# Two late modulation rows summed 256 columns at a time in the gate units; block means transposed straight from the gate tile

## What is computed

```python
mod = silu(c) @ w_ada + b_ada                     # 6 rows of 1,024
shift1, scale1, gate1, shift2, scale2, gate2 = split(mod, 6)
h  = modulated_norm(x, norm_mix_g, shift1, scale1)
xr, gr, zu, zv, ga, gb = split(h @ w_in, ...)
y_a = (rg_lru(conv4(xr)) * gelu(gr)) @ w_branch_a
v   = layernorm(gelu(zv))                         # over the channels of a token
y_b = (gelu(zu) * (blockwise 128x128 masked position mixing of v + b)) @ w_branch_b
x   = x + gate1 * ((sigmoid(ga) * y_a + sigmoid(gb) * y_b) @ w_out)
h   = modulated_norm(x, norm_ffn_g, shift2, scale2)
x   = x + gate2 * ((gelu(a) * b) @ w_down)        # a, b: conv3 of h @ w_up
return rmsnorm(x, norm_final_g)
```

## Time and profile before

| | |
|---|---|
| median of three runs | 1533.09 us (1532.81 to 1533.11) |
| the profiled execution | 1533.34 us, of which its span is 1531.6 us |
| PE | 1510.5 us busy, 99% of the span |
| DVE | 1199.9 us, 78% |
| ACT | 811.6 us, 53% |
| POOL | 387.0 us, 25% |
| granted TensorE clock | full in all slices |

### The profile page before, as it was taken

The page is one execution under the profiler, slowest core; times in us unless marked ns, Lnnn a source line. Parts: engine busy times, 40 slices in busy tenths (PEclk is TensorE's granted clock), DMA queues, the critical chain, the costliest instruction groups (busy, mean ns, idle before and its releaser), DMA issues.

```text
span 1531.6 us, 19518 instructions
## 1 busy us (share of the span) xinstructions
PE 1510.5 (99%) x6820; PEld 1243.1 (81%) x6820; DVE 1199.9 (78%) x1484; ACT 811.6 (53%) x1207; POOL 387.0 (25%) x291
## 2 busy tenths in 40 slices
PE   7999999999999999999999999999999999999998
PEld 4778888888888888888887788888888888888887
DVE  6987888745565685478859999999999987777775
ACT  5378988745554460112535555655555553444447
POOL 0024334522222200000000333333333331333324
PEclk9999999999999999999999999999999999999999
DMA  9531233222332256674421144444444446777722
GB/s 347 182 104 49 82 90 91 86 66 71 111 103 83 97 169 225 185 241 134 165 62 35 49 151 165 152 151 151 152 151 152 151 131 230 242 249 249 248 66 111
DMA packets 199985, 219.56 MB, mean 143 GB/s; under 512 B 8944, under 2 KB 155728, under 8 KB 199120
## 3 DMA queue, kind: packets, MB, share of 16 engines
q1 hardware_dynamic: 199888, 218.32, 43.1%
HBM read 160.61 MB, written 57.67 MB: 143 GB/s over the span
## 4 chain that ended last, share of the span: by engine, by line
PE 90%; DVE 7%; ACT 1%; issue 1%; DMA 0%; DVEq 0%; ACTq 0%
PE ps L808 70%; PE ps L881 10%; PE ps L1159 1%; PE ps L1068 1%; PE ps L1011 1%; PE ps L1141 1%; PE ps L931 1%; DVE wop L1838 1%; PE ps L966 1%; DVE part_acc L1901 1%; DVE yq L1936 1%; DVE hidw L2481 1%; DVE tn L1931 1%; DVE yq L2424 1%; DVE n L2416 0%
## 5 line engine op out<-in xcount | busy, mean ns | idle before, releaser
L1222 ACT ACTIVATE wop<-raw 128x512 fp32r<-128x512 f32 (+1 forms) x529 | 299.4, 570 | 401.2 <-PE ps L808 209.9
L1838 DVE TENSOR_TENSOR wop<-raw,wop 128x512 fp32r<-128x512 f32 (+1 forms) x529 | 366.9, 697 | 163.0 <-ACT wop L1222 161.0
L808 PE MATMUL ps<-yq,wop 128*128 128x512 f32 x1680 | 404.6, 390 | 1.3 <-DVE wop L1838 0.9
L808 PEld LDWEIGHTS ps<-yq,wop 128*128 128x128 f32 x1680 | 314.8, 188 | 69.2 <-DVE yq L2424 1.6
L649 POOL TENSOR_TENSOR raw<-raw,raw 128x512 f32<-128x512 f32 (+1 forms) x65 | 95.7, 1472 | 925.3 <-DVE wop L1838 428.6
L808 PE MATMUL ps<-dq,wop 128*128 128x512 f32 x840 | 190.6, 389 | 0.0
L808 PEld LDWEIGHTS ps<-dq,wop 128*128 128x128 f32 x840 | 157.7, 188 | 32.7
L1852 DVE TENSOR_TENSOR ps<-ps,snap_p 128x512 f32<-128x512 f32 x128 | 89.0, 696 | 56.2 <-PE ps L808 55.5
L808 PE MATMUL ps<-t2q,wop 128*128 128x512 f32 x528 | 127.7, 391 | 1.1 <-DVE wop L1838 1.1
L808 PE MATMUL ps<-t4q,wop 128*128 128x512 f32 x528 | 127.2, 390 | 1.0 <-DVE ps L1852 1.0
L808 PE MATMUL ps<-t3q,wop 128*128 128x512 f32 x528 | 127.8, 391 | 0.0
(11 more groups left out here) (266 smaller groups left out, 1979.9 us busy)
## 6 DMA issues: line engine op xcount, KB each, us to landing
dq<-hid_keep SPq DMA_DIRECT2D x35, 1024.0 KB, 7.2
raw<-in_w_in SPq DMA_DIRECT2D x96, 256.0 KB, 3.9
raw<-in_w_up SPq DMA_DIRECT2D x96, 256.0 KB, 3.3
hid_keep<-part_b SPq DMA_DIRECT2D x40, 512.0 KB, 3.0
ada_ring<-in_w_ada SPq DMA_DIRECT2D x32, 512.0 KB, 4.4
hid_keep<-part_t SPq DMA_DIRECT2D x20, 512.0 KB, 2.8
raw<-in_w_down SPq DMA_DIRECT2D x80, 128.0 KB, 2.3
ada_w<-in_w_ada SPq DMA_DIRECT2D x8, 1024.0 KB, 11.5
```

Source lines behind the costliest of these rows:

```text
L808: done = nc.tensor.matmul(bank, left[:, w, lk, :], right[:, x, rk, :], start=(first and w == 0 and x == 0), stop=(last and w == 1), skip_g ...
L1222: nc.scalar.activation(wop[n % 4][:, 0, 0:depth[n], :], raw[slot][:, 0:depth[n], :], ACT.Copy).then_inc(f_hi, 1)
L1838: V.tensor_tensor(wop[n % 4][:, 1, 0:kd, :], raw[slot_of[n][0]][:, 0:kd, :], wop[n % 4][:, 0, 0:kd, :].bitcast(F32), ALU.subtract).then_in ...
```

## The change

Rows 0 and 1 are no longer made in `A` 1 and `A` 2. They are cut into eight parts ("quarters" of a row) of 256 columns, one for each unit with a block b. In unit j of these, DVE sums eight pieces of 128x256 (`quarter_piece`), one or two behind the `lo` of each step. They come from a ring of four buffers of 128 KB, which lie where `vstage` was. PE sums the partitions of the quarter after product 1 of the next unit (two matmuls of one column), DVE adds the bias at w = 3 (`quarter_columns`), and PE waits for that (`mod_ready`) before it mixes. The transposes read `vv` itself, so `stage` and `vstage` are gone. Rows 2 and 3 stay in `B` 0 and `B` 1. SP issues the pieces between weight and gate transfers, and the first return of `ya_raw` moves behind the first weights of `ZU` 3 and also waits for the last quarter.

```diff
-        ADA_AT = {AT["A", 1]: 0, AT["A", 2]: 1, AT["B", 0]: 2, AT["B", 1]: 3}
-        SUMS_AT = {AT["A", 2]: 0, AT["A", 3]: 1, AT["B", 1]: 2, AT["B", 3]: 3}
+        ADA_AT = {AT["B", 0]: 2, AT["B", 1]: 3}
+        SUMS_AT = {AT["B", 1]: 2, AT["B", 3]: 3}
+        QUARTER_AT = {pos: V_BLOCK[pos] for pos in V_BLOCK}
...
+            def quarter_pieces(j, *ks):
+                for k in ks:
+                    n = KT * j + k
+                    if n == 0:
+                        sp.wait_ge(scanned, KT)
+                    if n >= len(quarter_ring):
+                        sp.wait_ge(ring_used, n + 2 - len(quarter_ring))
+                    slot = n % len(quarter_ring)
+                    sp.dma_start(quarter_ring[slot][:, :], w_ada[:, k, 2 * D + j * QC:2 * D + (j + 1) * QC])\
+                      .then_inc(ring_landed[slot], 16)
...
-                weights(pos, 0, 4 if pos == 2 else 2)
+                weights(pos, 0, 1)
+                if now - 1 in QUARTER_AT:
+                    quarter_pieces(QUARTER_AT[now - 1], 7)
...
+                if now in QUARTER_AT:
+                    quarter_pieces(QUARTER_AT[now], 0, 1, 2)
+                weights(pos, 1, 4 if pos == 2 else 2)
...
+                if now in QUARTER_AT:
+                    quarter_pieces(QUARTER_AT[now], 3)
                 if pos > 2:
                     weights(pos, 3, 4)
+                if now in QUARTER_AT:
+                    quarter_pieces(QUARTER_AT[now], 4, 5, 6)
...
+                if pos - 1 in QUARTER_AT:
+                    j = QUARTER_AT[pos - 1]
+                    if w == 2:
+                        pe.wait_ge(*outputs_read(pos - 1, 1))
+                        pe.wait_ge(*quarter_used(j, KT - 1))
+                        column_sums(quarter_acc, QC // P, past[1][:, 0, 0:QC // P]).then_inc(ada_psum, 1)
+                    if w == 4:
+                        pe.wait_ge(mod_ready, j + 1)
...
-                        pe.wait_ge(staged, b + 1)
+                        if b == 0:
+                            pe.wait_ge(zv_ready, KT)
                         for g in range(G):
-                            last = nc.tensor.transpose(blocks(past[0])[:, g, :], vstage[:, g, :], ident[:, :])
+                            last = nc.tensor.transpose(blocks(past[0])[:, g, :], vv[:, g, b * P:(b + 1) * P], ident[:, :])
...
+            FIRST_OPS = ((), (0,), (1, 2), (3,), (4,), (5,), (6, 7))
+            QUARTER_OPS = ((0,), (1, 2), (3,), (4,), (5,), (6,), (7,))
+
+            def quarter_piece(j, k):
+                n = KT * j + k
+                w, before = quarter_ring[n % len(quarter_ring)], quarter_ring[(n - 1) % len(quarter_ring)]
+                dve.wait_ge(ring_landed[n % len(quarter_ring)], 16 * (n // len(quarter_ring) + 1))
+                if k == 0:
+                    V.tensor_scalar(w[:, :], w[:, :], cact[:, 0:1], None, ALU.mult).then_inc(ring_used, 1)
+                else:
+                    dve.wait_ge(*quarter_used(j, k - 1))
...
+                    dst = quarter_acc if k == KT - 1 else w
+                    V.scalar_tensor_tensor(dst[:, :], w[:, :], cact[:, k:k + 1], before[:, :], ALU.mult, ALU.add)\
+                     .then_inc(ring_used, 1)
...
+                    if pos - 1 in QUARTER_AT and w == 3:
+                        quarter_columns(QUARTER_AT[pos - 1], past[1])
                     if w or m is None:
                         lo(n0 + w + 3)
+                    if pos in QUARTER_AT:
+                        for k in (QUARTER_OPS if QUARTER_AT[pos] else FIRST_OPS)[w]:
+                            quarter_piece(QUARTER_AT[pos], k)
```

More of the change, by code:

```diff
@@ L157, in build @@
         sq_o = place("sq_o", [S], F32, "T", 2 * TILE)
-        ada_ring = [[place("ada_ring0", [D], F32, "X", 6 * TILE), place("ada_ring1", [D], F32, "T", 3 * TILE)],
-                    [place(f"ada_ring{2 + i}", [D], F32, "H", 3 * QUAD + at * TILE) for i, at in enumerate((0, 1, 3))]]
-        ada_acc = [place("ada_acc0", [D], F32, "X", 7 * TILE), place("ada_acc1", [D], F32, "H", 3 * QUAD + 2 * TILE)]
+        ada_ring = [place(f"ada_ring{i}", [D], F32, "H", 3 * QUAD + at * TILE) for i, at in enumerate((0, 1, 3))]
+        ada_acc = place("ada_acc", [D], F32, "H", 3 * QUAD + 2 * TILE)
+        QC = 2 * P
+        quarter_ring = [place(f"quarter_ring{i}", [QC], F32, "H", 3 * QUAD + i * 4 * QC) for i in range(4)]
+        quarter_acc = place("quarter_acc", [QC], F32, "BD", 2 * KB)
         n22, n12 = (place(n, [KH, HALF], F32, "H", (i + 1) * QUAD) for i, n in enumerate(("n22", "n12")))
@@ L263, in build @@
         r_psum, sbias_ready = sem("r_psum"), sem("sbias_ready")
-        staged, v_psum, var_ready, sd_ready, vhat_ready, mix_psum, mixed_ready, zu_ready, yb_ready = (
-            sem(x) for x in ("staged", "v_psum", "var_ready", "sd_ready", "vhat_ready", "mix_psum", "mixed_ready",
+        v_psum, var_ready, sd_ready, vhat_ready, mix_psum, mixed_ready, zu_ready, yb_ready = (
+            sem(x) for x in ("v_psum", "var_ready", "sd_ready", "vhat_ready", "mix_psum", "mixed_ready",
                              "zu_ready", "yb_ready"))
@@ L270, in build @@
             sem(x) for x in ("yb_hi", "yb_lo", "ma_done", "mb_done", "mg_hi", "mg_lo"))
-        ring_landed, ring_used = [sem(f"ring_landed{s}") for s in range(3)], sem("ring_used")
+        ring_landed, ring_used = [sem(f"ring_landed{s}") for s in range(4)], sem("ring_used")
         ada_sum, ada_psum, mod_ready = (
@@ L312, in build @@
         V_BLOCK = {AT["G", 2 + b] if b < 6 else AT["ZU", b - 6]: b for b in range(NB)}
-        ADA_AT = {AT["A", 1]: 0, AT["A", 2]: 1, AT["B", 0]: 2, AT["B", 1]: 3}
-        SUMS_AT = {AT["A", 2]: 0, AT["A", 3]: 1, AT["B", 1]: 2, AT["B", 3]: 3}
+        ADA_AT = {AT["B", 0]: 2, AT["B", 1]: 3}
+        SUMS_AT = {AT["B", 1]: 2, AT["B", 3]: 3}
+        QUARTER_AT = {pos: V_BLOCK[pos] for pos in V_BLOCK}
+        QUARTERS = 2 * D // QC
+        EARLY = KT * QUARTERS
+        assert QUARTERS == len(QUARTER_AT)
         def plain(item):
@@ L393, in ring_place, with quarter_used @@
         def ring_place(e, k):
-            n = KT * (e % 2) + k
-            slots = len(ada_ring[e // 2])
-            return n % slots, 16 * (n // slots + 1 + (KT if e >= 2 and n % slots < 2 else 0))
+            n = KT * (e - 2) + k
+            return n % len(ada_ring), 16 * (n // len(ada_ring) + 1 + EARLY // len(quarter_ring))
+        def quarter_used(j, k):
+            return ring_used, KT * j + k + 1
         def prev_unit(pos, kind, back=1):
@@ L523, in _ @@
                 now = pos - 1
-                weights(pos, 0, 4 if pos == 2 else 2)
+                weights(pos, 0, 1)
+                if now - 1 in QUARTER_AT:
+                    quarter_pieces(QUARTER_AT[now - 1], 7)
+                if SEQ[now - 1] == ("ZU", 1):
+                    sp.wait_ge(mixed_ready, NB)
+                    sp.wait_ge(ring_used, EARLY)
+                    sp.wait_ge(ya_spilled[0], 16 * KT // 2)
+                    sp.wait_ge(ya_spilled[1], 16 * KT // 2)
+                    sp.dma_start(ya_raw[0][:, :, :], ya_keep[:, 0:KH, :]).then_inc(kept_back[0], 16)
+                if now in QUARTER_AT:
+                    quarter_pieces(QUARTER_AT[now], 0, 1, 2)
+                weights(pos, 1, 4 if pos == 2 else 2)
                 g = prev_unit(now, "G")
@@ L536, in _ @@
                 if now in ADA_AT:
-                    ada_pieces(ADA_AT[now], len(ada_ring[ADA_AT[now] // 2]), 7 if ADA_AT[now] == 3 else 8)
+                    ada_pieces(ADA_AT[now], len(ada_ring), 7 if ADA_AT[now] == 3 else 8)
                 if SEQ[now] == ("B", 2):
@@ L556, in _ @@
                       .then_inc(ws_landed, 16)
[L557 to L561, removed]
                 if SEQ[now] == ("ZU", 3):
@@ L1498, in _ @@
                             gate_tanh(1, 1)
-                        if b is not None and b + 1 < NB:
-                            stage(b + 1)
                         if SEQ[pos] == ("ZU", 3):
@@ L2052, in scan, with quarter_columns @@
                 V.tensor_tensor_scan(ti[m % 2][:, :], la_a[:, :], ti[m % 2][:, :], 0.0, ALU.mult, ALU.add).then_inc(scanned, 1)
+            FIRST_OPS = ((), (0,), (1, 2), (3,), (4,), (5,), (6, 7))
[8 more added lines that the diff above has]
+                    dve.wait_ge(*quarter_used(j, k - 1))
+                    if k == KT - 1 and j:
+                        dve.wait_ge(ada_psum, j)
+                    dst = quarter_acc if k == KT - 1 else w
+                    V.scalar_tensor_tensor(dst[:, :], w[:, :], cact[:, k:k + 1], before[:, :], ALU.mult, ALU.add)\
+                     .then_inc(ring_used, 1)
+            def quarter_columns(j, bank):
+                n, c0 = QC // P, 2 * KT + QC // P * j
+                dve.wait_ge(ada_psum, j + 1)
+                V.tensor_tensor(mod[:, c0:c0 + n], bank[:, 0, 0:n], C("b_ada", c0, n), ALU.add).then_inc(mod_ready, 1)
             def v_stats(b, bank):
@@ L2229, in _ @@
                         e = ADA_AT[pos]
```

(3 more changed lines are left out.)

45 lines of the change are left out of this document (17 added, 28 removed).

## The result

The changed kernel takes 1538.19 us (median of six runs, 1536.49 to 1539.89) against 1533.05 us (six runs, 1532.81 to 1533.37). The ratio is 1.0033, with a 95% interval of 1.0023 to 1.0043: slower by 5.1 us, where 5.75 us were forecast. The spread is new: 3.4 us, where the kernel before has 0.6.

What follows compares the result with a forecast made beforehand. PE, busy throughout 93 to 806 us, was taken as the bound. Column sums 0.2, `G` 2 1.8 and three late pieces 3.75 sum to 5.75 us: 1538.8 us from the 1533.09 median, range 1534.5 to 1543.0.

Steps and rivals of the forecast that it cites:

- What bounds the kernel: From 93 to 806 us PE alone bounds; DVE work removed gives nothing, added costs nothing until PE waits.
- Staging copy: ACT loses eight copies, none on the chain, hidden by busy PE: nothing.
- Column sums: On PE, eight small sums of 0.48 us (3.9 us) replace two costing 3.70: net +0.2 taken, up to +1.0 us.
- the line that I drew: PE column-sum cost from two sizes: 0.114 us a record plus 0.03 fixed, so 0.48 us for 4 records.
- Pieces of 0.48 us: Each 256-column DVE piece takes 0.48 us; two in w = 1 delay the variance 0.9 us, hidden by the root's table load.
- `G` 2, 1.8 us: Two pieces ahead of `vhat`, the second held up by POOL at the port: PE waits 1.8 us.
- Late pieces: In the seven later units, piece 3 landing after its turn lets POOL in: 1.25 us each, three counted, 3.75 us.
- SP's queue and `ya_raw`: SP's waits for earlier pieces and the first `ya_raw` going out some 5 us later are hidden: nothing.
- B: Rival: all pieces land in time, only `G` 2 waits: 1535.1 us; chance 0.24.
- C: Rival: the piece loses the port to POOL in every later unit, even when landed: 1543.8 us; chance 0.14.
- D: Rival: pieces don't shut POOL out, `G` 2 costs 0.85 us: 1534.2 us in all; chance 0.06.
- the ring order: DMA engines take descriptors in ring order, so piece 3 stands behind 1 MB of gate tiles; landings of 5.0 to 6.2 us.

Runs made afterwards that it cites:

- the fourth experiment: Changed kernel with only the first unit's order changed, pieces 1 and 2 of `G` 2 moved behind `vhat`: 1535.99 us.
- the third experiment: Changed kernel with SP issuing piece 3 ahead of both gate tiles instead of behind them: 1535.18 us.
- fifth experiments: Changed kernel with piece 3 moved behind `vhat` in the seven later units, `G` 2 left as it is: 1535.06 us.
- the last two: Changed kernel with POOL's sums waiting for `vhat`: 1535.57 us; piece 3 issued early, plus pieces 2 and 3 ahead of `vhat` in seven later units: 1544.47 us.

## Why the prediction was right, point by point

- **What bounds the kernel.** It held: 16 pieces of 1,024 columns and eight ACT copies went and gave nothing, and in the version with all pieces behind `vhat` the new DVE work cost nothing.
- **Staging copy, nothing.** Measured at 0.9999 (0.9990 to 1.0007).
- **Column sums, +0.2 to +1.0, taken 0.2.** 0.51 us each, not 0.48: +0.4. The fixed part at the end of a sum (0.17 us) stays whole at this size, and the small group's own part is 0.34, under the line that I drew.
- **Pieces of 0.48 us, those in w = 1 hidden.** Their mean lies at 0.48. In `G` 3 the root ran at 369.56, right behind the load of its table, 5.72 us after the first transposes as before the change, although the variance came 1.0 us later in its unit.
- **`G` 2, 1.8 us.** 1.68 in the chain, 1.6 between two experiments. The mechanism is shown four ways: one piece instead of two, none, POOL kept away, and the same order made in seven other units. The lower bound, 0.85 without blocking, is what `G` 2 costs with POOL kept away (0.83).
- **Late pieces, 1.25 us each, three of them.** Three of 1.14 us in the profiled execution. Which units was half wrong. I had `G` 4 and `G` 5 late and `G` 3 and `G` 6 close; `G` 3, `G` 5 and `G` 7 were late, and `G` 4 early by enough. The step that failed there is carrying each unit's landing time over from one execution. That the count came out at three is luck: the profiled execution of the fourth experiment, with the same transfers, had two. Behind POOL stood only two of the three; for `G` 5 the forecast had 0.3 us of lateness and POOL on top, and it was 1.24 us of lateness with next to nothing of POOL. The issue directly behind the tile and the landing some 0.3 us behind it were right: in `G` 5 the tile landed at 410.96 + 6.6 = 417.56 and the piece at 412.20 + 5.7 = 417.9.

```profile
gate_keep<-tg SPq DMA_DIRECT2D x1, 512.0 KB, 6.6
quarter_ring<-in_w_ada SPq DMA_DIRECT2D x1, 128.0 KB, 5.7
```

- **The spread.** I had not forecast it, though it follows from the same step: how late the pieces are, and how many of six, varies from run to run. That it comes from piece 3 is shown: where that piece is issued early or stands behind `vhat`, the runs spread by 0.6 to 1.3 us instead of 3.4. That the single times are counts of late pieces is not shown. With 1533.05 + 1.7 + 0.4 = 1535.15 us and 1.14 us for each late piece, one to four late pieces give 1536.3, 1537.4, 1538.6 and 1539.7 us, and the six runs were 1536.49, 1537.42, 1538.12, 1538.26, 1538.60 and 1539.89. But any time lies within 0.57 us of such a step, and only the profiled one, 1538.26, has a trace: three late pieces, where the sum gives 1538.6.
- **SP's queue and `ya_raw`, nothing.** No wait of PE in those units, in any version.
- **Rivals.** B is what the third and fifth experiments make (1535.18 and 1535.06, where 1535.1 stood). C and D are refuted, by the third experiment and by the last two. The traces agree with the Trainium skill's rule on the port (SBUF — State Buffer, "Who interferes with whom"): behind POOL a piece took 1.36 and 1.33 us instead of 0.48, and behind a piece POOL's sum took 1.47 us instead of 1.29. Of the two statements on transfers that the prediction takes from the Trainium skill (DMA: Bandwidth & Descriptors), the ring order fits the 4.9 and 5.7 us that the piece took behind the gate tiles. The section with the fixed part of about 2.0 us ("Anatomy of one DMA") is on transfers that GpSimd issues, and SP issues all of these; what the trace shows for SP is that pieces with no gate tile ahead of them, such as the one issued at 362.67, took 2.0 us and more.

## What to carry to other kernels

Work put in front of the one instruction that arrives just in time is not hidden, however idle the engine is on average: look for the smallest margin in the unit, and put fill-in work behind it. Two dependent instructions on VectorE open a gap in which GpSimd takes the port for a whole instruction, so the second costs far more than the first (1.3 us against 0.24 to 0.34 here). And a small transfer that is wanted soon should not be queued behind large ones that nobody waits for.

## What the runs showed of the hardware that was not expected

- A piece that landed 0.36 us late (`G` 3) and one that landed 1.21 us late (`G` 5) cost PE the same 1.14 us. While POOL's sum runs, it doesn't matter when in it the piece lands: behind both, `vhat` starts 2.46 us after the `lo` does, where it is 1.20 us with the piece in time (`G` 4). The second piece came just before the sum ended, and would have cost as much without it.
- The landing of the same 512 KB gate tile went 5.8, 4.9, 6.6, 4.9, 5.9 and 5.1 us from `G` 3 to `ZU` 0, up and down by turns, where it was 5.2, 6.2, 5.8, 5.5, 5.0 and 5.0 before. What sets it was not tried and stays open.
- PE loses up to 0.24 us at the 128-column matmuls of the mixing before a wait shows: it takes 1.78 us where `vhat` and `mod` are early, 1.80 and 1.96 us in two units of the kernel with POOL kept away, and 2.02 us wherever there is a gap in the chain, even one of 0.00 or 0.03 us.
